# Sample attention moved beside prompt attention, in plain fp32 on quarter arrays

## The chip, the core and the metric

The kernel runs on one core of one Trainium2 chip. Its engines work from queues of their own and wait for each other by semaphores: TensorE (PE, with its weight loads shown as PEld), VectorE (DVE), ScalarE (ACT), GpSimd (POOL) and SyncE (SP), which here issues nearly all DMAs. The metric is the device time of one execution in microseconds.

## The reference

A two-layer decoder trunk serves a prompt of 1024 new tokens and 8 sample requests of 4 new tokens each. Layer 0 is a causal convolution module, layer 1 is forgetting attention with 16 heads of 64; each is followed by a SwiGLU FFN. The change is in layer 1, behind the joint projection of q, k, v and the log forget values:

```python
def fox_prompt(q, k, v, logf):            # 1024 queries over 1024 keys, causal, blocks of 128 queries
    c = jnp.cumsum(logf, axis=1)
    s = einsum('bqhd,bkhd->bhqk', qi, k) * scale + ci[..., None] - cT[:, :, None, :]
    pr = softmax(where(kpos <= qpos, s, -inf)); return einsum('bhqk,bkhd->bqhd', pr, v)

def fox_sample(q, k, v, logf, cache_k, cache_v, cache_logf, page_table):
    kp = cache_k[page_table].reshape(DB, P, H, dh)    # 8 pages of 128 rows for each of 8 requests
    vp = cache_v[page_table].reshape(DB, P, H, dh)
    # the same attention of 4 new queries over 1024 cached rows and themselves
```

A cache page is 128 rows x 1024 values of fp32, 512 KB for the keys and as much for the values; 64 pages of each are read.

## The kernel before, in words

All work is laid out by hand: each engine has one queue, written in order, and waits where the code says so. The kernel goes through the stages one after the other: convolution, FFN, attention projection, prompt attention, sample attention, output projection, FFN, final norm. Projections multiply with operands split into a high and a low fp32r part (three products, lines 749 to 751). The weights of a projection pass through two buffers `wraw`; ACT casts each to `whi` (line 1184) and POOL subtracts it into `wlo` (line 655).

*Prompt attention* takes the 16 heads as 8 pairs, and each pair in 8 slots: query tiles of 128 rows, from tile 7 (1024 keys) down to tile 0 (128 keys). For slot n PE computes the scores of both heads, one on the upper and one on the lower 64 rows of the array (`scores_pair`, line 1024), into banks 0 to 3. DVE adds the cumulated log forget values and takes the negated row maximum in one instruction (`tile_max`, line 1823), POOL having put the causal mask on the diagonal block (line 714). ACT takes the exponential into `pr` (line 1458). In the next slot PE transposes `pr` block by block (`probs_tr`, line 995) into banks 4 and 5, from which DVE and ACT copy it to `pt` (lines 1814 and 1444). A slot later PE multiplies with the values (`values`, line 1041), each head in its own 64 columns of the array, into bank 6 or 7. When a half of a pair (four tiles) is done, the reciprocal sums are spread by a transpose (line 1007), copied to `R`, and applied on the way to `OT` (line 1831). The order of PE's queue and the last wait of `scores_pair` are

```python
            for n in range(NSLOT + 2):
                early = n < NSLOT and query_tile(n) < 3
                ... scores_pair(n), probs_tr(n - 1, 0), probs_tr(n - 1, 1), scale_tr ...
                if n >= 2:
                    values(n - 2)
                past(pe, a_exp, 2 * (n - 1) if qt < 3 else 2 * n)
```

where for the wide tiles `scores_pair` stands behind the first head's transposes, and for tiles 2 to 0 (`early`) ahead of them.

*Sample attention* starts when all of that is done (`sp.wait_ge(a_pv, NSLOT)`). Per request, the 8 key pages are loaded into four buffers `kr`, transposed on PE (line 1075), split into `KTh` by ACT (1480) and `KTl` by DVE (1877), and multiplied with queries spread over 64 rows, high and low part side by side (1088, 1089). The exponential (1510) is transposed (1105), split again, and multiplied with value pages split into `Vh` by ACT (1488) and `Vl` by POOL (722), in products of 128 x 512 (1116, 1117), 1122 adding the new tokens. Of the 64 x 1024 results PE selects each head's own columns (`select`, line 1130). The values of a request are taken while the keys of the next are. Then `OT` is split into `xhi` and `xlo` and the output projection starts. Its first two weight units have been loaded and split ahead.

Of the kernel before, what the change touches and what calls it, by code (L numbers as in the profile page):

```python
# [34 lines left out]
ds = bass.ds  # L35
# [5 lines left out]
def hybrid_step(nc, x_prompt, x_sample, state_conv, cache_k, cache_v, cache_logf, page_table,  # L41
# [35 lines left out]
    with ExitStack() as ctx:  # L77
# [83 lines left out]
        own = at("own", [P, C, H], F32, after("newqk"))  # L161
        isum = at("isum", [P, 64], F32, after("own"))
        NMT = at("NMT", [H * TNEW, NREQ, NS], F32, after("isum"))
# [11 lines left out]
        NM = at("NM", [NS, NREQ, H, TNEW], F32, after("csumt"))  # L175
# [5 lines left out]
        smx = at("smx", [H * TNEW, 1], F32, after("rden"))  # L181
        sden = at("sden", [H * TNEW, 1], F32, after("smx"))
        srd = at("srd", [P, 1], F32, after("sden"))
# [5 lines left out]
        qa = at("qa", [P, 2, SEQ], F32, where["xhi"][0])  # L189
        ka = at("ka", [P, 2, SEQ], F32, after("qa"))  # L190
        cb = at("cb", [P, 2, 2, SEQ], F32, after("ka"))
# [3 lines left out]
        pt = at("pt", [P, 2, 2, SEQ], F32, where["stg"][0])  # L195
# [7 lines left out]
        kr = at("kr", [P, 4, D], F32, where["stg"][0])  # L203
        assert after("kr") <= where["newqk"][0]
        KTh = at("KTh", [P, 2, C, 2 * P], FR, H0)
        KTl = at("KTl", [P, 2, C, 2 * P], FR, after("KTh"))
        assert after("KTl") <= where["kr"][0]
        vr = at("vr", [P, 2, D], F32, where["xhi"][0])

        vr2 = at("vr2", [P, 2, D], F32, where["wraw"][0])  # L210
        Vh = at("Vh", [P, 2, D], FR, after("vr"))
        Vl = at("Vl", [P, 2, D], FR, after("Vh"))

        cbx = at("cbx", [H * TNEW, PAST], F32, after("Vl"))

        qs = at("qs", [P, C, P], FR, after("cbx"))
        assert after("qs") <= where["xlo"][0]
        qx = at("qx", [P, C, H, TNEW], F32, where["NM"][0])

        S = at("S", [H * TNEW, PAST + NS], F32, where["rs"][0])  # L220
        Pm = at("Pm", [H * TNEW, PAST + NS], F32, where["sq"][0])
        PTs = at("PTs", [P, NPG, P], FR, where["tm"][0])
        PTn = at("PTn", [NS, P], F32, where["fz"][0])
        ob = at("ob", [P, D], F32, where["csumt"][0])
# [75 lines left out]
        x_mm = sem("x_mm")  # L300
        x_ev = sem("x_ev")
        a_ld = [sem("a_ld0"), sem("a_ld1")]
        a_sc = sem("a_sc")
        a_mask = sem("a_mask")
        a_mx = sem("a_mx")
        a_exp = sem("a_exp")
# [1687 lines left out]
```

## Time and profile before

| | |
|---|---|
| median of 3 runs | 3156.82 us (3156.65 to 3157.34) |
| the profiled execution | 3151.71 us, its span 3150.0 us |
| busy in the span | PE 2858.6 us (91%), DVE 1121.6, ACT 962.5, POOL 967.3 |
| mean granted TensorE clock | 0.953 of full speed |
| HBM | 191.48 MB read, 23.13 MB written |

A span is the time from the first to the last instruction that the profiler recorded. Busy times of matmuls are modelled, since they are pipelined: a matmul's row includes its way through the array, and the distance between the starts of two weight loads or matmuls tells what one costs in a stream. A plain fp32 matmul is recorded as two passes, so the counts of such rows are twice the matmuls. "Idle before <- releaser" is the time that an engine had stood idle ahead of a row, and who ended it. [...]

### The profile page before, as it was taken

How to read it: one execution, taken by the hardware profiler on the slowest of the kernel's cores; microseconds unless marked ns; L12 is line 12 of the kernel's file. 1: busy time of each engine (PE TensorE's matmuls, PEld its weight loads, DVE VectorE, ACT ScalarE, POOL GpSimd, SP SyncE). 2: the span in 40 equal slices, each digit the busy share in tenths (PEclk: the TensorE clock that was granted, in tenths of full speed). 3: DMA queues.
4: the chain of work that ended last, by engine and by line, in shares of the span. 5: the costliest groups of instructions: out<-in, count | busy, mean ns of one | idle time of the engine just before them, and what ended most of it. 6: DMA issues, size and time to landing. Idle time of an engine off the chain costs nothing.

```text
span 3150.0 us, 48571 instructions
## 1 busy us (share of the span) xinstructions
PE 2858.6 (91%) x17970; PEld 2661.0 (84%) x17970; DVE 1121.6 (36%) x1820; ACT 962.5 (31%) x1549; POOL 967.3 (31%) x564
## 2 busy tenths in 40 slices
PE   5887698999999999899988888998989999999997
PEld 4787497999999999799975556886879999999997
DVE  6999634111111112511126665553351111111114
ACT  4555523211112112302124544554232111111123
POOL 2899323222222222312112212556131221212211
PEclk8898799999999999999999998988899999999998
DMA  3101011111111111224222114775111111111111
GB/s 97 40 27 40 15 47 34 37 50 47 34 54 37 50 47 34 62 70 129 72 74 110 55 55 166 275 251 189 41 38 42 40 47 43 44 47 36 52 36 72
DMA packets 244634, 215.16 MB, mean 68 GB/s; under 512 B 18108, under 2 KB 218812, under 8 KB 243492
## 3 DMA queue, kind: packets, MB, share of 16 engines
q1 hardware_dynamic: 231399, 194.98, 19.7%
q10 hardware_dynamic: 13133, 18.80, 1.8%
q8 instruction: 65, 1.06, 0.1%
q14 instruction: 37, 0.30, 0.0%
HBM read 191.48 MB, written 23.13 MB: 68 GB/s over the span
## 4 chain that ended last, share of the span: by engine, by line
PE 74%; DVE 15%; issue 5%; ACT 3%; DMA 1%; POOL 1%; DVEq 0%; SPq 0%; ACTq 0%; POOLq 0%
PE PS L749 20%; PE PS L751 20%; PE PS L750 20%; DVE PS L1685 6%; PE PS L1024 3%; DVE tm L1574 2%; PE PS L995 2%; PE PS L1041 1%; PE PS L1075 1%; DVE rs L1553 1%; PE PS L1116 1%; PE PS L1117 1%; PE PS L1088 1%; PE PS L1089 1%; DMA xin<-in_x_prompt 1%
## 5 line engine op out<-in xcount | busy, mean ns | idle before, releaser
L749 PE MATMUL PS<-xhi,whi 128*128 128x352 f32 x3456 | 1144.0, 331 | 118.3 <-DVE u L1663 40.5
L751 PE MATMUL PS<-xlo,whi 128*128 128x352 f32 x3456 | 1120.8, 324 | 0.0
L750 PE MATMUL PS<-xhi,wlo 128*128 128x352 f32 x3456 | 1120.7, 324 | 0.0
L655 POOL TENSOR_TENSOR wlo<-wraw,whi 128x1024 fp32r<-128x1024 f32 x208 | 496.9, 2390 | 1605.6 <-ACT whi L1184 1605.6
L749 PEld LDWEIGHTS PS<-xhi,whi 128*128 128x128 f32 x3456 | 657.4, 190 | 161.9 <-DVE hlo L1616 48.1
L750 PEld LDWEIGHTS PS<-xhi,wlo 128*128 128x128 f32 x3456 | 660.4, 191 | 0.0
L751 PEld LDWEIGHTS PS<-xlo,whi 128*128 128x128 f32 x3456 | 658.2, 190 | 0.0
L1184 ACT ACTIVATE whi<-wraw 128x1024 fp32r<-128x1024 f32 x208 | 218.9, 1052 | 595.4 <-PE PS L751 566.9
L1611 DVE TENSOR_TENSOR ht<-PS,ht 128x352 f32<-128x352 f32 x132 | 69.1, 524 | 906.1 <-PE PS L751 902.1
L749 PE MATMUL PS<-hhi,whi 128*128 128x352 f32 x1056 | 341.2, 323 | 8.8 <-issue 8.8
L750 PE MATMUL PS<-hhi,wlo 128*128 128x352 f32 x1056 | 338.5, 321 | 0.0
L751 PE MATMUL PS<-hlo,whi 128*128 128x352 f32 x1056 | 338.2, 320 | 0.0
L1597 DVE TENSOR_TENSOR X<-PS,X 128x352 f32 x216 | 113.2, 525 | 445.8 <-PE PS L751 445.4
L749 PEld LDWEIGHTS PS<-hhi,whi 128*128 128x128 f32 x1056 | 198.1, 188 | 10.8 <-issue 10.8
L750 PEld LDWEIGHTS PS<-hhi,wlo 128*128 128x128 f32 x1056 | 198.4, 188 | 0.0
L751 PEld LDWEIGHTS PS<-hlo,whi 128*128 128x128 f32 x1056 | 197.9, 187 | 0.0
L1685 DVE SCALAR_TENSOR_TENSOR PS<-u,par,PS 128x1024 f32<-128x1024 f32 x152 | 195.9, 1289 | 4.8
L722 POOL TENSOR_TENSOR Vl<-vr,Vh 128x1024 fp32r<-128x1024 f32 x64 | 151.7, 2384 | 137.2 <-ACT Vh L1488 137.2
L1239 ACT ACTIVATE hhi<-ht 128x352 f32 x132 | 65.5, 498 | 410.3 <-DVE ht L1611 410.3
L677 POOL TENSOR_TENSOR yp<-yp,prods 128x1024 f32<-128x1024 f32 x72 | 172.3, 2393 | 10.3
L1233 ACT ACTIVATE ht<-PS 128x352 f32<-128x352 f32 x132 | 60.8, 464 | 367.5 <-PE PS L751 367.4
L1286 ACT ACTIVATE prods<-u,par 128x1024 f32<-128x1024 f32 x88 | 99.6, 1149 | 113.2 <-POOL yp L677 68.8
(198 smaller groups left out, 2816.1 us busy)
## 6 DMA issues: line engine op xcount, KB each, us to landing
wraw<-in_ffn_w_gu SPq DMA_DIRECT2D x88, 512.0 KB, 3.8
kr<-in_cache_k SPq DMA_DIRECT2D x64, 512.0 KB, 5.1
vr<-in_cache_v SPq DMA_DIRECT2D x64, 512.0 KB, 5.1
wraw<-in_ffn_w_down SPq DMA_DIRECT2D x32, 384.0 KB, 3.3
wraw<-in_attn_w_in SPq DMA_DIRECT2D x24, 512.0 KB, 3.9
wraw<-in_ffn_w_down SPq DMA_DIRECT2D x32, 320.0 KB, 3.0
wraw<-in_conv_w_in SPq DMA_DIRECT2D x16, 512.0 KB, 4.0
cb<-c_scr SPq DMA_DIRECT2D x8, 1024.0 KB, 7.6
```

The source lines that it names most:

```text
L655: nc.gpsimd.tensor_tensor(wlo[:, s, :], wraw[:, s, :], whi[:, s, :].bitcast(F32), ALU.subtract).then_inc(w_lo, 1)
L677: nc.gpsimd.tensor_tensor(yp[:, :], prods[:, 0, :] if i == 1 else yp[:, :], prods[:, i % 3, :], ALU.add).then_inc(p_tap, 1)
L722: nc.gpsimd.tensor_tensor(Vl[:, j % 2, :], raw_values(j), Vh[:, j % 2, :].bitcast(F32), ALU.subtract).then_inc(v_lo, 1)
L749: nc.tensor.matmul(out, wh, hi[:, k, blk(b)], start=(k == 0), stop=False)
L750: nc.tensor.matmul(out, wl, hi[:, k, blk(b)], start=False, stop=False)
L751: m = nc.tensor.matmul(out, wh, lo[:, k, blk(b)], start=False, stop=(k == kc - 1))
L1024: m = nc.tensor.matmul(PS[:, score_banks(n, s) + k0 // 512, 0:k1 - k0], qa[rows, i % 2, qt * P:(qt + 1) * P], ka[rows, i % 2, k0:k1], star ...
L1184: nc.scalar.activation(whi[:, s, :], wraw[:, s, :], ACT.Copy).then_inc(w_hi, 1)
L1286: nc.scalar.activation(prods[:, i % 3, :], u[:, k:k + SEQ], ACT.Copy, scale=par[:, q, R_DW + k:R_DW + k + 1]).then_inc(a_tap, 1)
L1597: nc.vector.tensor_tensor(xs, PS[:, NB * s + b, 0:BW], xs, ALU.add).then_inc(ev[s], 1)
L1611: nc.vector.tensor_tensor(ht[:, b, :], PS[:, NB + b, 0:BW], ht[:, b, :], ALU.mult).then_inc(ev[1], 1)
L1685: nc.vector.scalar_tensor_tensor(acc, u[:, k:k + SEQ], tap(k), acc, ALU.mult, ALU.add).then_inc(cv, 1)
```

## The change

The sample stage goes, and its work is put into the prompt slots, in steps: step m transposes key page m, takes the scores of page m - 1, and the value products of page m - 11 (`LAG`). A slot does one step, the seventh slot of each pair two: 72 steps in the 64 slots, 4 more behind them. The splits are gone. Scores and values are plain fp32 matmuls on 32 columns of the array: four groups g of 32 columns hold the 16 heads, 4 heads by 4 new tokens in a group, with two matmuls (e = 0, 1) accumulated per group for the scores of a page, and one per group for its values (256 columns). Banks 4 and 5 are now filled alternately by a list (`fills`) that holds the prompt transposes (P), the spread sums (R), page scores (S, SN for the new tokens), the two halves of a page's transposed keys (K), the transposed probabilities of a request (T, TN) and the selection (O); a fill waits until the fill two places ahead has been copied out, by DVE or by ACT as listed. `pt` has one buffer in place of two, and `values(n - 1)` runs in slot n in place of `values(n - 2)`. Of two buffers for the queries of a pair one is left, and of two for its keys one and a half. The key pages (three buffers), the value pages (two) and `cbx` lie where `wraw`, `whi` and `wlo` are, so the weights of the output projection are loaded when the last key page has been transposed, and cast when the last value product is done. The transposition of the new tokens' mask, 8 transposes, becomes 32 small fp32 matmuls.

PE's queue, for the 768-key tile of the third head pair, from its scores to the value products of the tile before. Before:

```order
L1024 MATMUL PS<-ka,qa 128x512 [waits a_exp]
L1024 MATMUL PS<-ka,qa 128x512
L1024 MATMUL PS<-ka,qa 128x256 x2
L995 MATMUL PS<-ident,pr 128x128 [waits a_ptv,a_exp]
L995 MATMUL PS<-ident,pr 128x128 x3
L995 MATMUL PS<-ident,pr 128x128 [waits a_pta]
L995 MATMUL PS<-ident,pr 128x128 x2
L1041 MATMUL PS<-pt,Vt 64x128 [waits a_pta,a_ptv,o_ev]
L1041 MATMUL PS<-pt,Vt 64x128 x15
```

After, from the second half of the second head's transposes on (ahead of it stand the same scores, now from `kl` and `kh`):

```order
L1035 MATMUL PS<-ident,pr 128x128 [waits a_pta]
L1035 MATMUL PS<-ident,pr 128x128 x2
L1102 MATMUL PS<-KT,qs 32x128 [waits a_pta,a_ptv]
L1102 MATMUL PS<-KT,qs 32x128 x7
L1121 MATMUL PS<-ident,kr 128x128 [waits a_pta,k_ld2]
L1121 MATMUL PS<-ident,kr 128x128 x3
L1121 MATMUL PS<-ident,kr 128x128 [waits a_ptv]
L1121 MATMUL PS<-ident,kr 128x128 x3
L1133 MATMUL PS<-vr,PT 32x256 [waits v_ld1]
L1133 MATMUL PS<-vr,PT 32x256 x3
L1085 MATMUL PS<-pt,Vt 64x128 [waits a_pta,a_ptv]
L1085 MATMUL PS<-pt,Vt 64x128 x13
```

Behind the probabilities there are now, ahead of the value products, the page scores (KT, qs), both halves of the key transposes (kr), of which the second waits for DVE (a_ptv), and the page values (vr, PT).

DVE's queue in the same slot. Before:

```order
L1814 COPY pt<-PS 128x512 [waits a_pv,a_tr]
L1823 ISA PS,nmx<-PS,cb 128x768 [waits a_mask,a_sc]
L1823 ISA nmx 128x1
L1814 COPY pt<-PS 128x512 [waits a_pv,a_tr]
L1823 ISA PS,nmx<-PS,cb 128x768 [waits a_mask,a_sc]
L1823 ISA nmx 128x1
```

After (smx and S are the running maximum and the scores of the request):

```order
L1838 COPY pt<-PS 128x512 [waits a_pv,a_tr]
L1847 ISA PS,nmx<-PS,cb 128x768 [waits a_mask,a_sc]
L1847 ISA nmx 128x1
L1847 ISA PS,nmx<-PS,cb 128x768 [waits a_mask,a_sc]
L1847 ISA nmx 128x1
L1881 ISA S,smx<-PS,cbx 128x128 [waits a_tr]
L1881 ISA smx 128x1
L1902 COPY KT<-PS 128x512 [waits a_tr] x2
```

The second copy of probabilities has moved to ACT, and behind both maxima stand the exit of the page's scores and the two copies of its transposed keys.

```diff
+        kr = at("kr", [P, 3, D], F32, where["wraw"][0])
+        vr = at("vr", [P, 2, D], F32, after("kr"))
+        cbx = at("cbx", [P, PAST], F32, after("vr"))
+        assert after("cbx") <= where["xhi"][0]
+        KT = at("KT", [P, C, P], F32, after("cb"))
+        assert after("KT") <= where["xlo"][0]
...
+        NPAGE = NREQ * NPG
+        LAG = NPG + 3
+        NSTEP = NPAGE + LAG + 1
+        NALL = NSLOT + 4
+        def steps_before(n):
+            return n + min(n // NT + (1 if n % NT > 6 else 0), C)
+        def sample_steps(n):
+            return range(steps_before(n), min(steps_before(n + 1), NSTEP))
...
+        def fills():
+            for n in range(NALL):
+                if 1 <= n <= NSLOT:
+                    wide = query_tile(n - 1) >= 4
+                    yield ("P", n - 1, 0, 0), ON_DVE
+                    if wide:
+                        yield ("P", n - 1, 0, 1), ON_ACT
+                    yield ("P", n - 1, 1, 0), ON_ACT
+                    if wide:
+                        yield ("P", n - 1, 1, 1), ON_ACT
+                    if halves_ended(n - 1):
+                        yield ("R", (n - 1) // 4), ON_DVE
+                for m in sample_steps(n):
+                    if 1 <= m <= NPAGE:
+                        yield ("S", m - 1), ON_DVE
+                        if (m - 1) % NPG == 0:
+                            yield ("SN", (m - 1) // NPG), ON_DVE
+                    if m < NPAGE:
+                        yield ("K", m, 0), ON_DVE
+                        yield ("K", m, 1), ON_DVE
...
+        def bank(key):
+            return 4 + fill[key] % 2
+        def emptied(eng, u):
+            engine, n = filled_by[u]
+            eng.wait_ge(a_ptv if engine == ON_DVE else a_pta, n)
...
+            def load_k(p):
+                if p >= 3:
+                    bank_full(sp, ("K", p - 3, 1))
+                v = page(p)
+                sp.dma_start(kr[:, p % 3, :], cache_k[0][ds(v, 1)].rearrange("a p h d -> p (a h d)")
+                             ).then_inc(k_ld[p % 3], 16)
+            def load_v(p):
+                if p >= 2:
+                    sp.wait_ge(v_mm, p - 1)
+                v = page(p)
+                sp.dma_start(vr[:, p % 2, :], cache_v[0][ds(v, 1)].rearrange("a p h d -> p (a h d)")
+                             ).then_inc(v_ld[p % 2], 16)
...
                 if n % 4 == 0:
-                    past(pe, o_ev, hh - 1)
+                    past(pe, o_ev, hh)
                 for kb in range(qt + 1):
                     for s in range(2):
-                        m = nc.tensor.matmul(PS[DH * s:DH * s + DH, 6 + hh % 2, (qt % 4) * P:(qt % 4 + 1) * P],
+                        m = nc.tensor.matmul(PS[DH * s:DH * s + DH, 6, (qt % 4) * P:(qt % 4 + 1) * P],
                                              Vt[:, kb, i * P + s * DH:i * P + s * DH + DH],
-                                             pt[:, n % 2, s, kb * P:(kb + 1) * P],
+                                             pt[:, s, kb * P:(kb + 1) * P],
                                              start=(kb == 0), stop=(kb == qt))
                 m.then_inc(a_pv, 1)
-            for n in range(NSLOT + 2):
+            def page_scores(p):
+                b, j = divmod(p, NPG)
+                if j == 0:
+                    pe.wait_ge(d_q, b + 1)
+                evacuated(pe, ("K", p, 0))
+                evacuated(pe, ("K", p, 1))
+                u = ("S", p)
+                bank_free(pe, u)
+                for e in range(2):
+                    for g in range(4):
+                        m = nc.tensor.matmul(PS[NS * g:NS * g + NS, bank(u), 0:P], qs[:, b % 2, 2 * g + e, :],
+                                             KT[:, 2 * g + e, :], start=(e == 0), stop=(e == 1))
+                m.then_inc(a_tr, 1)
...
+            def page_tr(p):
+                pe.wait_ge(k_ld[p % 3], 16 * (p // 3 + 1))
+                for half in range(2):
+                    u = ("K", p, half)
+                    bank_free(pe, u)
+                    for c in range(4):
+                        m = nc.tensor.transpose(PS[:, bank(u), c * P:(c + 1) * P],
+                                                kr[:, p % 3, (4 * half + c) * P:(4 * half + c + 1) * P], ident[:, :])
+                    m.then_inc(a_tr, 1)
+            def page_values(p):
+                b, j = divmod(p, NPG)
+                if j == 0:
+                    evacuated(pe, ("TN", b))
+                    past(pe, d_ob, b)
+                pe.wait_ge(v_ld[p % 2], 16 * (p // 2 + 1))
+                for g in range(4):
+                    m = nc.tensor.matmul(PS[NS * g:NS * g + NS, 7, 0:2 * P], PT[:, j, NS * g:NS * g + NS],
+                                         vr[:, p % 2, 2 * P * g:2 * P * (g + 1)], start=(j == 0), stop=False)
...
+                m.then_inc(v_mm, 1)
...
+            def sample_step(m):
+                if 1 <= m <= NPAGE:
+                    page_scores(m - 1)
+                if m < NPAGE:
+                    page_tr(m)
+                if LAG <= m < NPAGE + LAG:
+                    page_values(m - LAG)
+                if m >= LAG - 1 and (m - LAG + 1) % NPG == 0 and m - LAG + 1 < NPAGE:
+                    sample_tr((m - LAG + 1) // NPG)
+                if m >= LAG + NPG and (m - LAG) % NPG == 0:
+                    select((m - LAG) // NPG - 1)
+            for n in range(NALL):
                 early = n < NSLOT and query_tile(n) < 3
                 if early:
                     scores_pair(n)
@@ -1056,107 +1189,13 @@
                     probs_tr(n - 1, 1)
                     if halves_ended(n - 1):
                         scale_tr((n - 1) // 4)
-                if n >= 2:
-                    values(n - 2)
+                for m in sample_steps(n):
+                    sample_step(m)
+                if 1 <= n <= NSLOT:
+                    values(n - 1)
...
+            act.wait_ge(v_mm, NPAGE)
+            for s in range(2):
+                hi_part(Q_ATTN_OUT, s)
+            evacuated(act, ("O", NREQ - 1))
...
-                for a, u in enumerate(tr_units(n)[s]):
-                    if u % 2:
-                        continue
-                    dve.wait_ge(a_tr, u + 1)
-                    past(dve, a_pv, n - 1)
-                    k0, k1 = 512 * a, min(nk, 512 * a + 512)
-                    nc.vector.tensor_copy(pt[:, n % 2, s, k0:k1], PS[:, 4 + u % 2, 0:k1 - k0]).then_inc(a_ptv, 1)
+                u = tr_units(n)[s][0]
+                bank_full(dve, u)
+                past(dve, a_pv, n)
+                k1 = min(nk, 512)
+                nc.vector.tensor_copy(pt[:, s, 0:k1], PS[:, bank(u), 0:k1]).then_inc(a_ptv, 1)
...
+            def page_out(p):
+                b, j = divmod(p, NPG)
+                u = ("S", p)
+                bank_full(dve, u)
...
+                nc.vector.tensor_tensor_reduce(S[:, b % 2, j * P:(j + 1) * P], PS[:, bank(u), 0:P],
+                                               cbx[:, j * P:(j + 1) * P], 1.0, -3.0e38, ALU.add, ALU.max,
+                                               accum_out=smx[:, b % 2, j:j + 1]).then_inc(a_ptv, 1)
...
+            def keys_in(p):
+                if p >= 1:
+                    bank_full(dve, ("S", p - 1))
+                for half in range(2):
+                    u = ("K", p, half)
+                    bank_full(dve, u)
+                    nc.vector.tensor_copy(KT[:, 4 * half:4 * half + 4, :],
+                                          PS[:, bank(u), :].rearrange("p (c f) -> p c f", f=P)).then_inc(a_ptv, 1)
...
+            for n in range(NALL):
+                ended = 1 <= n <= NSLOT and halves_ended(n - 1)
+                if 1 <= n <= NSLOT:
+                    probs_out(n - 1, 0)
...
+                if n < NSLOT:
+                    for s in range(2):
+                        tile_max(n, s)
+                if ended:
+                    bank_full(dve, ("R", hh))
+                    past(dve, o_ev, hh)
+                    nc.vector.tensor_copy(R[:, :], PS[:, bank(("R", hh)), :]).then_inc(a_ptv, 1)
+                if 2 <= n < NSLOT + 2 and halves_ended(n - 2):
+                    half_out((n - 2) // 4)
+                for m in sample_steps(n):
+                    sample_step(m)
...
```

## Rows read from the trace of the kernel before

**Rows 1.** Windows: engines' busy us (instructions), granted clock, DMA share, GB/s.
```profile
1629.74:1919.20 289.46, 246.71 (x2165) 164.54 (x2165) 176.71 (x407) 145.03 (x360) 56.77 (x126) 0.97 0.16 62
1919.20:2217.48 298.28, 269.18 (x1654) 225.18 (x1653) 141.29 (x172) 146.40 (x165) 151.73 (x64) 0.83 0.69 236
1776.09:1811.28 35.19, 30.03 (x273) 20.23 (x273) 22.13 (x52) 18.04 (x46) 7.20 (x16) 1.00 0.16 61
2000.00:2150.00 150.00, 145.44 (x926) 123.67 (x925) 80.35 (x96) 79.86 (x90) 83.90 (x36) 0.87 0.77 266
```

**Rows 2.** Waits of DVE and ACT, prompt stage: us in total, times, longest.
```profile
DVE PS L1823 <- PE PS L1024: 76.5, 48, 4.5
...
ACT pr L1458 <- DVE nmx L1823: 106.8, 79, 3.9
```

**Rows 3.** Timeline, one turn of a 768-key tile: start us, us, engine, instructions.
```profile
1680.38 1.56 PE L1024 MATMUL PS<-ka,qa 64*128 64x512 f32 x8 [0.57 <-ACT pr L1458]
1681.87 0.75 PEld L995 LDWEIGHTS PS<-ident,pr 128*128 128x128 f32 x7 [0.33 <-issue]
1681.97 0.97 DVE L1823 CUSTOM_DVE_ANT_0 PS<-PS,cb 128x768 f32<-128x768 f32 x1 [1.64 <-PE PS L1024]
1682.79 1.73 PEld L1041 LDWEIGHTS PS<-pt,Vt 128*64 128x64 f32 x32 [0.17 <-issue]
1682.86 0.69 DVE L1814 COPY pt<-PS 128x512 f32<-128x512 f32 x1
1683.46 0.96 DVE L1823 CUSTOM_DVE_ANT_0 PS<-PS,cb 128x768 f32<-128x768 f32 x1
1684.33 0.14 DVE L1823 DVE_READ_ACCUMULATOR2_ANT nmx<- 128x1 f32 x1
1684.51 0.90 ACT L1458 ACTIVATE pr<-PS,nmx 128x768 f32<-128x768 f32 x1
1685.31 0.19 ACT L1458 ACTIVATION_READ_ACCUMULATOR pr<-PS,nmx 128x1 f32 x1
1685.55 0.30 PEld L1024 LDWEIGHTS PS<-ka,qa 64*128 64x128 f32 x4 [0.23 <-ACT pr L1458]
```

**Rows 4.** Groups by line and shape, prompt stage: count, busy us, mean ns.
```profile
L1823 DVE CUSTOM_DVE_ANT_0 PS<-PS,cb 128x1024 f32<-128x1024 f32 x16 | 19.6, 1230 | 12.4 <-PE PS L1024 12.4
L1444 ACT ACTIVATE pt<-PS 128x512 f32<-128x512 f32 x24 | 14.3, 594 | 24.2 <-PE PS L995 24.2
L1823 DVE CUSTOM_DVE_ANT_0 PS<-PS,cb 128x128 f32<-128x128 f32 x16 | 4.7, 294 | 3.9 <-PE PS L1024 3.9
```

**Rows 5.** Timeline: scores of 1024 and 128 keys, four transposes and their copy.
```profile
1629.74 1.99 PE L1024 MATMUL PS<-ka,qa 64*128 64x512 f32 x8 [1.33 <-DVE NMT L1793]
...
1672.21 0.66 PE L995 MATMUL PS<-ident,pr 128*128 128x128 f32 x4 [1.30 <-ACT pr L1458]
1672.90 0.69 DVE L1814 COPY pt<-PS 128x512 f32<-128x512 f32 x1 [0.65 <-PE PS L995]
...
1700.34 0.49 PE L1024 MATMUL PS<-ka,qa 64*128 64x128 f32 x4
```

**Rows 6.** Timeline, PE: undivided passes of small and of large matmuls.
```profile
1617.92 1.03 PE L932 MATMUL PS<-ident,newqk 128*32 128x128 f32 x8 [0.40 <-ACT Vt L1408]
...
1627.97 0.44 PE L982 MATMUL PS<-ident,NM 32*64 32x32 f32 x8
...
2042.67 1.98 PE L1122 MATMUL PS<-vnew,PTn 32*128 32x512 f32 x4
```

**Rows 7.** Timeline: the first output-projection matmul.
```profile
2217.48 0.63 PE L749 MATMUL PS<-xhi,whi 128*128 128x352 f32 x1 [1.68 <-DVE xlo L1946]
```

**Rows 8.** DMA issues: KB each, median us to landing.
```profile
kr<-in_cache_k SPq DMA_DIRECT2D x64, 512.0 KB, 5.1
```

**Rows 9.** Groups by line: cast of a weight unit and its low part.
```profile
L655 POOL TENSOR_TENSOR wlo<-wraw,whi 128x1024 fp32r<-128x1024 f32 x208 | 496.9, 2390 | 1605.6 <-ACT whi L1184 1605.6
L1184 ACT ACTIVATE whi<-wraw 128x1024 fp32r<-128x1024 f32 x208 | 218.9, 1052 | 595.4 <-PE PS L751 566.9 <-DMA wraw<-in_attn_w_in 25.7 <-DMA wraw<-in_conv_w_in 2.8
```

More of the change, by code:

```diff
@@ L406, in score_banks, with evacuated, bank_free, bank_full @@
             return 2 * s + (1 if qt in (2, 0) else 0)
-        def evacuated(eng, u):
-            if u >= 0:
-                eng.wait_ge(a_ptv if u % 2 == 0 else a_pta, u // 2 + 1)
+        fill, filled_by, count = {}, [], [0, 0]
+        for key, engine in fills():
+            count[engine] += 1
+            fill[key] = len(filled_by)
+            filled_by.append((engine, count[engine]))
+        def bank(key):
[3 more added lines that the diff above has]
+            eng.wait_ge(a_ptv if engine == ON_DVE else a_pta, n)
+        def evacuated(eng, key):
+            emptied(eng, fill[key])
+        def bank_free(eng, key):
+            if fill[key] >= 2:
+                emptied(eng, fill[key] - 2)
+        def bank_full(eng, key):
+            eng.wait_ge(a_tr, fill[key] + 1)
+        def tr_units(n):
+            return [[("P", n, s, a) for a in range(2 if query_tile(n) >= 4 else 1)] for s in range(2)]
         def banks(first, n):
@@ new lines, in select @@
+            def select(b):
+                u = ("O", b)
+                pe.wait_ge(d_ob, b + 1)
+                bank_free(pe, u)
+                for e in range(2):
+                    m = nc.tensor.matmul(PS[:, bank(u), NS * e:NS * e + NS], ob[:, e * P:(e + 1) * P],
+                                         ident[:, :].rearrange("p (g x) -> p g x", g=4)[:, :, 8 * e:8 * e + 8],
+                                         start=True, stop=True)
+                m.then_inc(a_tr, 1)
+            def sample_step(m):
[5 more added lines that the diff above has]
+                    page_values(m - LAG)
+                if m >= LAG - 1 and (m - LAG + 1) % NPG == 0 and m - LAG + 1 < NPAGE:
+                    sample_tr((m - LAG + 1) // NPG)
+                if m >= LAG + NPG and (m - LAG) % NPG == 0:
+                    select((m - LAG) // NPG - 1)
@@ L1079, in scores @@
-            def scores(b, g):
-                pe.wait_ge(k_lo, b * NPG + (2 * g + 2))
-                if g == 0:
-                    pe.wait_ge(d_q, b * 2 + 2)
-                    past(pe, d_s, b * 4)
-                out = PS[:, 4 + g // 2, (g % 2) * 2 * P:(g % 2 + 1) * 2 * P]
-                for c in range(C):
-                    nc.tensor.matmul(out, qs[:, c, :], KTh[:, g % 2, c, :], start=(c == 0), stop=False)
-                    m = nc.tensor.matmul(out, qs[:, c, :], KTl[:, g % 2, c, :], start=False, stop=(c == C - 1))
-                m.then_inc(k_sc, 1)
@@ L1150, in _ @@
-            request(0, False, False)
-            request(1, True, False)
-            with pe.Fori(2, NREQ) as b:
-                request(b, True, True)
-            select(NREQ - 2)
-            exp_tr(NREQ - 1)
-            for j in range(NPG):
-                values_page(NREQ - 1, j)
-            select(NREQ - 1)
-            pe.wait_ge(d_o, 2 * NREQ)
+            evacuated(pe, ("O", NREQ - 1))
             def attended(b, k):
```

573 lines of the change are left out of this document (231 added, 342 removed).

## The prediction

> **What bounds the kernel now.** I read the page's forty slices first, then the stages by window, then who waits for whom in the first of them, then one turn of its loop in the timeline. Two stages are touched. Prompt attention runs from 1629.74 to 1919.20 us and sample attention from there to 2217.48, where the first output-projection matmul starts: 289.5 + 298.3 = 587.7 us [rows 1, 7]. In the sample stage PE shows busy for 269 of 298 us: PE-bound, at a mean granted clock of 0.83. In the prompt stage no engine is full, DVE has 177 of 289 us and ACT 145. There DVE's row maxima wait 76.5 us for the scores and ACT's exponentials 106.8 us for the maxima [rows 2]: a chain of handovers. One turn shows it [rows 3]: scores of the 768-key tile start at 1680.38, the two maxima at 1681.97 and 1683.46, the second exponential is read out at 1685.50, and only then (1685.55) do the next scores start. 5.17 us a turn; PE's transposes and value products lie inside the waits. So the prompt stage has room on every engine, and the question is what order the new work takes in it.
>
> **The change, part by part.** *Removed:* the separate sample stage, 298.3 us, with the hi/lo splits of keys and values on ACT, DVE and POOL. *Added to each prompt turn:* one page step on PE (page scores, 8 key transposes, page values), on DVE one score exit and two key copies. ACT gets one exponential and three copies per request. There are 64 slots and 72 page steps in them (the seventh slot of each pair has two), then four closing steps.
>
> What an added PE pass costs. A plain fp32 matmul shows two passes. With 512 moving columns and the array not divided by columns, a pass starts each 0.43 us (four in 1.98 us with the tail) [rows 6], so 0.107 us per 128 columns. The value products, in two column halves, take 32 passes of 128 columns in 1.73 us, 0.054 us each [rows 3]: two run side by side. No row shows four side by side. The lower end is four: 0.027 us per 128-column pass, and 32-column passes do start about 0.036 us apart, (0.44 - 0.19)/7 with 0.19 the tail of one [rows 6]. The upper end is one at a time: 32-column weights by themselves take 0.107 us per pass, eight in 1.03 us with the tail [rows 6]. Nothing excludes a value between; I take the end nearest the half-array row, four, with page scores 16 x 0.032 = 0.5 us and page values 8 x 0.054 = 0.43 us. One at a time each would be 1.72 us. [...]
>
> Where it lies. Three orders decide. PE now issues, per turn: first-head transposes, scores, second-head transposes, page scores, key halves K0 and K1, page values, value products of the tile before. All fills of banks 4 and 5 alternate strictly, so K1 waits until DVE has taken the page's scores out. And DVE takes them out behind both maxima. So the loop closes anew: scores, max, max, score exit, K1, page values, value products, first-head transposes, scores. The exponentials, which closed the loop before, get cover. Behind the waiting K1 in PE's queue stand the page values, the value products and the next scores, and for those wait DVE and ACT.
>
> The closing run per step, at the higher clock: score exit 0.29 us plus the accumulator read, 0.35 in all [rows 4]; hop 0.05; four key transposes 4 x 0.107 = 0.43; change of array division 0.17 (the idle time ahead of the value products [rows 3]); page values 0.43; 0.17; value products 0.216 per key block of the tile before; 0.17; transposes 0.107 per block; 0.2 to the scores (0.23 in [rows 3]). Without the two block terms that is 1.97. Ahead of it: scores to first maximum 1.59 us at 768 keys, one step of 128 keys 0.215 (1.99 us of scores at 1024, 0.49 at 128 [rows 5]); two maxima, 1.23 us each at 1024 and 0.29 at 128 [rows 4], less the 0.08 overlapped with the read.
>
> In three slots of eight (768, 640 and 512 keys) the page scores are late, not the maxima: they wait for ACT's copy of the second head, which for 768 starts 1.49 + 0.69 us after the scores ([rows 3]; four transposes to their copy in [rows 5]), takes 0.59 [rows 4], and is followed by 0.17 + 0.5 + 0.27 of page scores: exit at about 3.8 us instead of 3.4. Where a half ends, a copy of R or the OT product (0.69 us each) stands in DVE's queue ahead of the exit.
>
> Slot by slot from 1024 to 128 keys I get 8.1, 9.1, 7.9, 7.4, 6.7, 6.7, 7.8 (two page steps) and 4.4 us: 58.1 per pair, against 35.19 at full clock now [rows 1]. The present stage takes 289.46/8 = 36.18 per pair, a factor 1.028 for dips of the clock; so 59.7. Pair 0 has no page values yet (9 x 0.6 less: 54.3), pair 1 two fewer (58.5), five pairs at 59.7, and the last has no key page left and stays near the old loop, 40: together 451. Per request once: 9 transposes 0.96, their three alternating fills behind ACT 0.9, scores of the new tokens 0.35, selection 0.6, exponential, reciprocal and copies about 0.7 in queue: 3.5 x 8 = 28. Start: 32 small matmuls in place of 8, and DVE now waits for the store of the cumulated sums before its first maximum: 3 us. End: values of page 63 can only be loaded when page 61 has been used; a page takes 5.1 us to land [rows 8], and behind the last product stand the first weight cast, 1.05 us, and POOL's difference, 2.39 [rows 9], no longer done ahead because their buffers hold pages: 10.5 us. In all 451 + 28 + 3 + 10.5 = 492.5 us in place of 587.7.
>
> Costed at nothing: page loads. Keys are issued three pages ahead and values about two turns ahead, against 5.1 us to land; 1 MB per turn of 7 us is 150 GB/s where the sample stage moved 236 [rows 1]. Without that cover each page would add up to 5 us. POOL's mask (0.46 us) stays inside the maxima. Later stages are the same code.
>
> Sum: 3151.71 - 95 = 3056.7 us for an execution like the profiled one; the median of the runs, 3156.82, is 5.1 above it, so 3062.
>
> **Rivals.**
> *Quarter arrays only two at a time.* Then page scores and values take 0.86 us each: 0.43 on the loop, and of the other 0.36 about 0.14 a step on average, since only three slots wait for it. 0.57 x 64 = 37 us later: 3099. For it: the trace shows a factor of two and no more. Against: 32-column passes can start every 0.036 us.
> *One at a time, slower than before.* 1.29 us more page values on the loop, 1.2 more page scores of which the maxima cover a third: 2.1 x 64 = 134 us, 3196. It wins over the gain from 95/64 = 1.5 us a page on. Against: the half tiles do overlap; for: weights of 32 columns alone bring nothing in [rows 6].
> [...]
> *More is hidden than I count.* If the request work fits the waits and the page scores never decide, 28 + 10 us go: 3024.
>
> **How the numbers follow.** Main forecast 0.62; two at a time 0.11; clock 0.11; more hidden 0.08; one at a time 0.05; other ways to be slower (a page load uncovered, a clock of 0.8 or below) 0.03. The likeliest alone spans 3035 to 3095, from a loop 5% shorter or longer (22 us) and 10 us in the ends. The range 3015 to 3130 takes in the first three rivals that make it faster. A time within 0.2% (6.3 us), about what a measurement of this kernel can tell from no change, needs nearly the whole gain lost: 0.03. Faster 0.89, slower 0.08.
>
> **What would show it.** Right: no sample stage behind prompt attention; 58 to 61 us from one 1024-key score to the next in the middle pairs; PE's second key half waiting for DVE's 128-column score exit, and ACT no longer the one that releases the scores; page values 0.45 to 0.6 us a page; the first output-projection matmul near 2122 us; about 10 us between the last prompt tile and it. Wrong: page values near 0.9 or 1.7 us; PE waiting for a page's DMA in the middle; a granted clock under 0.9 in the stage; a pair under 54 us or over 64.

## The result: 2.3% faster, some 20 us short of the forecast

The changed kernel takes 3082.85 us (median of 4 runs, 3079.12 to 3089.54) against 3157.08 us for the kernel before, timed beside it: a ratio of 0.9767, 95% interval 0.9749 to 0.9786. The forecast was 3062 us; 95 us were to go, 74 went. The profiled execution lasts 3085.33 us, its span 3083.2 us.

A stage is counted here from its own first prompt scores, which the kernels below reach at 1627.3 to 1633.5 us, to the first output-projection matmul. Windows of the changed kernel, columns as in [rows 1]: the whole stage, then the third, the fifth and the sixth pair of heads (from first 1024-key scores to first 1024-key scores), and the end, from the first value products behind the last slot on.

```profile
1633.48:2147.73 514.25, 425.31 (x4520) 279.10 (x4521) 273.89 (x706) 178.65 (x433) 59.82 (x128) 0.94 0.52 175
...
1756.51:1829.42 72.91, 60.24 (x616) 39.25 (x615) 36.12 (x94) 22.98 (x56) 7.43 (x16) 0.88 0.52 170
...
1894.50:1959.08 64.58, 53.84 (x598) 35.53 (x598) 35.74 (x92) 21.69 (x53) 7.19 (x16) 0.97 0.52 184
1959.08:2019.91 60.83, 52.81 (x598) 34.63 (x597) 35.55 (x92) 21.68 (x53) 7.19 (x16) 1.00 0.59 194
...
2134.80:2147.73 12.93, 5.89 (x41) 2.06 (x41) 3.90 (x8) 4.01 (x8) 2.88 (x2) 0.50 0.45 137
```

The two stages of [rows 1] took 587.7 us together; the one stage takes 514.3 where 492.5 were forecast. The row that answers to [rows 7] starts at 2147.73 (forecast "near 2122"); 3.7 us of the difference lie ahead of the stage. From the transposes of the new tokens, which are the same in both kernels, to the first scores it is 11.83 us here and 11.82 before (1617.92 in [rows 6], 1629.74 in [rows 5]):

```profile
1621.65 1.03 PE L970 MATMUL PS<-ident,newqk 128*32 128x128 f32 x8 [0.40 <-ACT Vt L1447]
...
1633.48 1.13 PE L1067 MATMUL PS<-kl,qa 64*128 64x512 f32 x4 [1.03 <-DVE NMT L1819]
```

Against the forecast, with the 3.5 us of a request in each pair: start 0.0 us (3), pair 0 55.4 (57.8), pair 1 67.7 (62.0), pairs 2 to 6 together 328.7 (316.0), the last 49.6 (43.5), end 12.9 (10.5). So pairs 1 to 6 lack 18 us, the last one 6.

First, a slot that nothing disturbs. Timeline of the changed kernel, the 896-key tile of pair 4 (columns as in [rows 3]):

```profile
1902.64 1.13 PE L1067 MATMUL PS<-kl,qa 64*128 64x512 f32 x4
...
1904.44 1.10 DVE L1847 CUSTOM_DVE_ANT_0 PS<-PS,cb 128x896 f32<-128x896 f32 x1 [1.44 <-PE PS L1067]
...
1905.46 1.13 DVE L1847 CUSTOM_DVE_ANT_0 PS<-PS,cb 128x896 f32<-128x896 f32 x1
...
1905.78 0.64 PE L1102 MATMUL PS<-KT,qs 128*32 128x128 f32 x16 [0.34 <-ACT pt L1485]
...
1906.51 0.68 DVE L1855 TENSOR_TENSOR OT<-PS,R 128x512 f32<-128x512 f32 x1
...
1907.11 0.28 DVE L1881 CUSTOM_DVE_ANT_0 S<-PS,cbx 128x128 f32<-128x128 f32 x1
...
1907.46 0.66 PE L1121 MATMUL PS<-ident,kr 128*128 128x128 f32 x4 [0.45 <-DVE smx L1881]
...
1908.04 0.64 PE L1133 MATMUL PS<-vr,PT 128*32 128x256 f32 x8
...
1911.43 1.13 PE L1067 MATMUL PS<-kl,qa 64*128 64x512 f32 x4
```

8.79 us from scores to scores, forecast 9.1. The second key half (L1121) waits for the score exit (L1881), which stands behind both maxima and the OT product: the loop of the forecast, in its order. The page values (L1133) last 0.64 us with their tail, and ACT no longer releases the scores, as it did in [rows 3].

Now where the time is. Waits of PE in the stage (us in total, times, longest):

```profile
PE PS L1121 <- DVE smx L1887: 23.6, 8, 5.5
PE PS L1121 <- DVE R L1960: 12.8, 12, 1.8
PE PS L1102 <- ACT pt L1485: 9.8, 22, 0.6
PE PS L1102 <- DVE pt L1838: 8.5, 21, 0.4
PE PS L1133 <- DMA vr<-in_cache_v: 5.9, 3, 3.6
PE PS L1121 <- DVE smx L1881: 5.5, 12, 0.5
```

The first row is in no term of the forecast: eight waits, one for each request, for the exit of its new-token scores (L1887), which stands behind the exit of its first page (L1881). Timeline of the changed kernel at one of them, ahead of the fourth request:

```profile
1809.22 0.29 DVE L1881 CUSTOM_DVE_ANT_0 S<-PS,cbx 128x128 f32<-128x128 f32 x1
...
1811.01 0.33 SPq L594 DMA_DIRECT2D kr<-in_cache_k  x1
1811.39 2.66 SPq L610 DMA_DIRECT2D cbx<-cb_scr  x4
...
1811.93 0.34 PE L1110 MATMUL PS<-newqk,qs 128*32 128x32 f32 x16
...
1817.34 0.29 DVE L1881 CUSTOM_DVE_ANT_0 S<-PS,cbx 128x128 f32<-128x128 f32 x1 [6.10 <-issue]
...
1817.79 1.94 PE L1121 MATMUL PS<-ident,kr 128*128 128x128 f32 x8 [5.52 <-DVE smx L1887]
```

The exit adds the request's cumulated log-forget sums, and cbx holds those of one request. Its reload may begin only when the last page of the request before has left (1809.22). SP gets to it behind a key page, 1.9 us after that exit has ended, and issues four transfers one after the other (2.66 us); DVE goes on 5.95 us after the first was issued. The new request's scores have been in PSUM since 1812.3; DVE waits, PE behind it. The profile names no releaser for this wait ("issue"). Of the seven waits of this kind in the stage it names the transfer for the two short ones (DVE's waits; us in total, times, longest):

```profile
DVE S L1881 <- issue: 19.5, 5, 6.1
...
DVE S L1881 <- DMA cbx<-cb_scr: 2.6, 2, 1.4
```

That it is the transfer in the other five too is an inference up to here, which the first experiments test. After the wait, in which PE stood for 5.5 us, the eight key transposes take 1.94 us, against 1.14 in an undisturbed slot: the granted clock is down, 0.50 from 1817.8 to 1819.8, 0.88 over this pair, 1.00 over pair 5.

### The profile page after: what moved, and what is told of

Same layout as the page of the kernel before. It is cut to its first block, busy times and chain, and to the rows that moved or that the text cites. A ratio compares the mean times of both kernels' runs of the same rounds, so it can differ in the third digit from the quotient of the medians.

```text
span 3083.2 us, 49477 instructions
## 1 busy us (share of the span) xinstructions
PE 2770.7 (90%) x18730; PEld 2554.4 (83%) x18730; DVE 1079.6 (35%) x1948; ACT 847.5 (27%) x1453; POOL 817.3 (27%) x500
## 4 chain that ended last, share of the span: by engine, by line
PE 75%; DVE 16%; issue 4%; ACT 3%; DMA 1%; POOL 1%; SPq 0%; DVEq 0%; ACTq 0%; POOLq 0%
PE PS L787 21%; PE PS L789 20%; PE PS L788 20%; DVE PS L1709 6%; PE PS L1067 2%; PE PS L1085 2%; PE PS L1121 2%; DVE tm L1598 2%; PE PS L1035 2%; DVE rs L1577 1%; PE PS L1133 1%; DVE PS L1847 1%; PE PS L1102 1%; DMA xin<-in_x_prompt 1%; DVE hlo L1640 1%
## 5 line engine op out<-in xcount | busy, mean ns | idle before, releaser
L763 POOL TENSOR_TENSOR cb<-cb,cmask 128x128 f32<-128x128 f32 x128 | 57.8, 459 | 449.7 <-DVE nmx L1847 440.8
L1485 ACT ACTIVATE pt<-PS 128x512 f32<-128x512 f32 (+3 forms) x128 | 57.7, 476 | 287.6 <-PE PS L1035 287.6
```

## The experiments

### The sums loaded once, and loaded in halves

One kernel loads for the first request alone. The other loads all, in two halves of the columns:

```
                 if b >= 1:
-                    evacuated(sp, ("S", b * NPG - 1))
+                    evacuated(sp, ("S", b * NPG - 1 - NPG // 2 * (1 - half)))
...
+                if p % NPG == 7 and (p + 1) // NPG < NREQ:
+                    load_sums((p + 1) // NPG, 0)
                 if p % NPG == 3 and 1 <= p // NPG < NREQ:
-                    load_sums(p // NPG)
+                    load_sums(p // NPG, 1)
...
-                    dve.wait_ge(cb_ld, 64 * (b + 1))
+                    dve.wait_ge(cb_ld[j // 4], 64 * (b + 1))
```

Once: 

> The four transfers that fill cbx are issued for the first request alone; the other seven use its sums (their sample outputs are other numbers). Theory, the reload of cbx is the missed term: in the changed kernel DVE stands 1.2 to 6.1 us ahead of the first page-score exit of each request, and PE 23.6 us in 8 waits for that exit. All of it goes and nothing else is late in its place: 20 to 35 us off, 3048 to 3063 us. Rival, the slots with two steps are long because PE's and DVE's queues hold more work there (new-token scores, transposes of the probabilities, the scale rows), and the transfer lands beside it: within 8 us of the changed kernel, 3075 to 3085 us.

Halves: 

> cbx is filled in two halves: columns of pages 0 to 3 as soon as page 3 of the request before has left it, four steps ahead of their use, columns of pages 4 to 7 where the whole was filled; 8 transfers of 32 KB a request instead of 4 of 64 KB, nothing left out. Theory, the reload is the missed term: the first half has some 25 us and the second one some 25 us of cover, so as much is gained as by no reload, within 6 us of that kernel (3050 to 3068 us). Rival, what costs is the SP queue that issues them, not the wait for the single buffer: four more issues a request of some 0.65 us each ahead of page loads, 3080 to 3095 us.

Measured: 3054.42 us, ratio 0.9689 (0.9673 to 0.9705), and 3052.89 us, 0.9677 (0.9661 to 0.9693). The intervals lie wholly below that of the changed kernel; the halves take 0.0090 x 3157 = 28 us off. The stage with the halves:

```profile
1627.77:2117.36 489.59, 415.76 (x4521) 272.78 (x4521) 273.30 (x706) 178.43 (x433) 59.66 (x128) 0.97 0.54 184
```

PE's waits in it:

```profile
PE PS L1125 <- DVE R L1965: 12.8, 12, 1.8
PE PS L1106 <- ACT pt L1489: 9.8, 22, 0.6
PE PS L1137 <- DMA vr<-in_cache_v: 9.8, 6, 3.7
PE PS L1106 <- DVE pt L1842: 8.7, 21, 0.4
...
PE PS L1125 <- DVE smx L1892: 2.9, 6, 1.0
```

The wait for the new-token exit goes from 23.6 to 2.9 us, the stage from 514.3 to 489.6, 2.9 us under the forecast, and its clock from 0.94 to 0.97, as forecast. Of the 24.7 us 15.1 are PE's idle time (20.7 us less at this exit, 3.9 more for value pages), and 9.6 its busy time, for the same work (4520 and 4521 records): that part goes with the clock. The reload is the missed term; the rival (longer queues in the slots with two steps) is out.

### The value products in one column group

```
-                    m = nc.tensor.matmul(PS[NS * g:NS * g + NS, 7, 0:2 * P], PT[:, j, NS * g:NS * g + NS],
+                    m = nc.tensor.matmul(PS[0:NS, 7, 0:2 * P], PT[:, j, NS * g:NS * g + NS],
...
```

The products of the new tokens are changed in the same way.

> The value products of the pages and of the new tokens all write the same 32 rows of the bank, added up over the four groups (the sample outputs are other numbers); in the changed kernel each of the four has 32 rows of its own. Theory, the four quarter arrays run at once: 16 passes of 256 columns one behind the other are 4 x 0.43 = 1.7 us a page instead of 0.43, and they stand in the loop of a slot, so 64 x 1.3 = 83 us slower where all of it shows and 40 where half is hidden: 3120 to 3170 us. Rival, the groups run one after the other already: within 5 us of the changed kernel.

Measured: 3157.80 us, 1.0011 (1.0002 to 1.0021): 77 us slower than the changed kernel, so the whole gain gone by this one edit. PE, the same eight passes (a plain fp32 matmul is two records: the 64 x 4 page matmuls of L1133 are 512 in either kernel, the 576 value products of L1041 in the kernel before 1152):

```profile
1912.15 1.91 PE L1133 MATMUL PS<-vr,PT 128*32 128x256 f32 x8
```

1.91 us in place of 0.64; 72 times (8 for the new tokens) 1.27 are 91 us, of which 77 show. One pass takes 0.22 us here (in the page before, the eighth starts 1.54 us behind the first); the last lasts 0.38. Two in a row would so end after 0.22 + 0.38 = 0.60 us (an estimate), and 0.64 is what the four groups take side by side. So four run at once, to within 0.04 us.

### Nothing beside prompt attention

```
         def steps_before(n):
-            return n + min(n // NT + (1 if n % NT > 6 else 0), C)
+            return NSTEP if n > NSLOT + 2 else 0
...
```

SP's loads follow that order: the prompt's first, then the pages.

Apart: 

> All 76 steps of sample attention stand behind the last query tile of prompt attention, in the same form (plain fp32, quarter arrays, the same buffers); nothing runs beside prompt attention. Theory, the gain comes from standing beside it: the prompt stage goes back to some 290 us, and the steps alone are bound by the page loads, 1 MB a page at the 236 GB/s of the sample stage before, 4.4 us x 64 = 284 us and some 36 for the requests: 3140 to 3180 us, about the kernel before. Rival, the form alone is the gain (no split of keys and values into parts, a page step of some 3 us: copies 0.69 x 2, scores 0.5, exit 0.3, products 0.43): 64 x 3 + 36 = 228 us, 3090 to 3100 us.

Apart, with the sums in halves: 

> All steps of sample attention behind prompt attention as before, with the sums loaded in halves. In the run with the whole reload DVE stood 51.3 us in 6 waits and 5.7 us in one ahead of a request's first exit, and PE 42.6 us for value pages. Theory, the page loads are the bound of steps that stand alone: part of the 57 us of the reload turns into waits for pages; 64 MiB of pages at 300 GB/s are 224 us instead of the 298 of the stage, with the prompt stage at 330: 3130 to 3165 us. Rival, the steps run at the 2.73 us of the undisturbed ones, 76 x 2.73 = 207 us and 4 us a request: 3110 to 3130 us.

Measured: 3207.09 us, 1.0177 (1.0154 to 1.0201), and 3192.15, 1.0131 (1.0110 to 1.0152). Both slower than the kernel before, and further than either theory said. The prompt stage and the sample stage of the second:

```profile
1627.26:1959.60 332.34, 257.01 (x2179) 173.48 (x2180) 160.08 (x383) 154.53 (x385) 56.37 (x126) 0.93 0.18 65
1959.60:2254.32 294.72, 196.37 (x2345) 124.72 (x2342) 116.60 (x324) 24.41 (x47) 2.88 (x2) 0.83 0.69 234
```

PE's longest wait in the latter:

```profile
PE PS L1130 <- DMA vr<-in_cache_v: 68.7, 40, 3.3
```

Two things follow. Standing alone, the new form of sample attention is hardly faster than the old (294.7 against 298.3 us): it has less to compute (PE 196.4 us busy against 269.2) and waits for its value pages instead, and its end holds the first weight cast, which the kernel before had done ahead. That its mean rate, 234 GB/s, is near the 236 of [rows 1] says nothing by itself, since both move the same pages in nearly the same time, and from 2040 to 2050 us this run moves 317 GB/s. Whether the rate or the short lead of two value buffers sets the wait was not tested. And the new prompt order by itself is 43 us slower than the old, 332.3 against 289.5. Some 10 us of that are PE's busy time (257.0 against 246.7, at a clock of 0.93 in place of 0.97), the rest waits. Those between 1700 and 1900 us, in the first of the two kernels, say where:

```profile
PE PS L1078 <- DVE OT L1848: 19.4, 10, 2.0
PE PS L1078 <- ACT pt L1478: 14.5, 20, 0.8
```

Its value products (L1078) wait for two things, 29.2 and 24.1 us over the whole prompt stage. They have one bank (6) where the kernel before had two (6 and 7), so a half of a pair begins only when DVE's OT product has emptied it; and they follow their own tile's transposes at once and wait for the copies, where before they were those of the tile before. The kernel before shows no wait of its value products (L1041) in that stage. This is read from the traces and was not tested by itself. So all of the gain comes from standing beside: 332.3 + 294.7 = 627.1 us apart become 489.6 beside.

### What closes the loop

On top of the halves. Maxima over 512 keys: `nk = min((query_tile(n) + 1) * P, 512)` in the maxima alone.

> As the kernel with the halves, but the maxima and the added bias take only the first 512 keys of a tile (the prompt outputs are other numbers). Theory of the forecast, both maxima of a slot stand in the loop that sets its length (scores, max, max, score exit, second key half): 2 x (1250 - 711) ns less in a slot of 1024 keys, 0.81, 0.54 and 0.28 us in those of 896, 768 and 640, 2.7 us a pair, 21 us in all: 3031 us. Rival, PE is the bound and what it waits for between the tiles is the scalar engine's last copy of pt, which gives the bank of the page scores back (0.45 us ahead of them in a slot of 768 keys); the maxima run beside: 3048 to 3056 us.

Score exit between the maxima:

```
                 if n < NSLOT:
-                    for s in range(2):
-                        tile_max(n, s)
+                    tile_max(n, 0)
                 if ended:
...
+                if between:
+                    for m in sample_steps(n):
+                        if 1 <= m <= NPAGE:
+                            page_out(m - 1)
+                if n < NSLOT:
+                    tile_max(n, 1)
```

> As the kernel with the halves, but in the slots with one step DVE takes the exit of the page scores between the two maxima, and R's copy ahead of it; the amount of work is the same. Theory of the forecast, the second maximum leaves the loop: 1.25, 1.12, 0.98, 0.85, 0.71, 0.58 and 0.31 us in the seven slots of a pair, up to 46 us off; half of it where something else is next: 3007 to 3030 us. Rival, the page scores are not there when the first maximum ends (in a slot of 768 keys they end 0.06 us behind the second one), so DVE waits for them with the second maximum behind, which has some 4 us before the next slot's transposes need it: 3046 to 3060 us.

Page scores ahead of the second head's transposes on PE, exit between the maxima on DVE:

```
+                if ahead(n):
+                    page_scores(ahead(n) - 1)
                 if 1 <= n <= NSLOT:
                     probs_tr(n - 1, 1)
```

> As the kernel with the halves, but in slots with one step (those of a request's first page left out) PE takes the page scores between the prompt scores and the transposes of the second head's probabilities, and DVE their exit between the two maxima; the order in which the two banks rotate follows. Theory, PE is the bound: its wait of 0.45 us for the copy of pt and of 0.2 us for the score exit go in each wide slot, and a wait of up to 0.3 us for the exit comes ahead of the second head's second block: 0.3 to 0.5 us in some 48 slots, 15 to 25 us off: 3028 to 3040 us. Rival, the loop through the maxima: the second maximum leaves it as well, over 30 us off: below 3020 us. Rival on the other side, the two banks now hold the score exit ahead of the transposes and every slot waits for DVE there: 3055 to 3080 us.

Measured: 3037.84 us, 0.9639 (0.9621 to 0.9656); 3041.37, 0.9650 (0.9630 to 0.9670); 3041.97, 0.9647 (0.9629 to 0.9665). Against the halves 12, 9 and 9 us by the ratios; the first interval lies under that of the halves, the other two overlap it. The stages of the profiled runs shrink by 19.1, 13.7 and 12.8 us. With the short maxima PE's waits are these:

```profile
PE PS L1106 <- ACT pt L1489: 9.8, 22, 0.6
PE PS L1137 <- DMA vr<-in_cache_v: 9.5, 5, 3.6
PE PS L1106 <- DVE pt L1842: 8.7, 21, 0.4
PE PS L1125 <- DVE R L1965: 6.4, 12, 0.8
```

The maxima are on the loop in part: 19.1 of 21 us in the profiled stages, 12 by the ratios, and 6.4 us of it are less wait for R's copy, which stands behind the maxima. The waits for the copies of pt (18.5 us in 43) don't move. The exit between the maxima, with R's copy moved as well (its wait falls to 5.7 us), gains far less than the 46 us of a second maximum, since the page scores aren't there yet. DVE at a 640-key tile of that kernel:

```profile
1891.62 0.83 DVE L1851 CUSTOM_DVE_ANT_0 PS<-PS,cb 128x640 f32<-128x640 f32 x1 [0.80 <-PE PS L1071]
...
1893.65 0.29 DVE L1886 CUSTOM_DVE_ANT_0 S<-PS,cbx 128x128 f32<-128x128 f32 x1 [1.14 <-PE PS L1106]
```

Neither theory holds by itself: two chains, maxima to score exit and pt's copies to page scores, end close to each other (0.06 us in the slot of 768 keys that the expectation names), so taking one away shows the other. The third edit shortens both, and new waits come in their place. PE's waits with the page scores ahead:

```profile
PE PS L1134 <- DVE R L1979: 5.6, 12, 0.6
...
PE PS L1060 <- DVE smx L1897: 4.7, 6, 0.8
...
PE PS L1115 <- DVE pt L1853: 3.7, 9, 0.4
PE PS L1134 <- ACT pt L1500: 3.3, 12, 0.4
```

At the page scores (L1115) PE waits 4.6 us for copies of pt in place of 18.5, and 5.6 in place of 12.8 for R's copy; but it now waits 3.3 us for ACT's copies at the key transposes (L1134) and 4.7 for the score exit at the spreading of the sums (L1060). That the two chains limit each other is read from these rows; no run takes both away.

With R's copy ahead of the second maximum too: 

> As the kernel with the page scores ahead, but in the slots that end a half of eight tiles DVE takes R's copy ahead of the second maximum too. Theory, PE is the bound of the stage and waits 5.6 us in 12 turns and 1.9 us in two for R's copy, in which the second maximum stands ahead of it by 0.7 or 1.25 us: 4 to 8 us less than the kernel with the scores ahead, 3034 to 3038 us. Rival, the second maximum is late then and with it the second head's exponentials, and the second head's transposes wait for them: 3040 to 3046 us.

Measured: 3046.74 us, 0.9655 (0.9642 to 0.9668): no gain over 0.9647. The rival held, in effect; where its time went was not followed further.

### The lead of the page loads

On top of the halves, two key buffers in place of three (`load_k` waits for page p - 2, not p - 3), and then the same with `load_v` ahead of `load_k` in SP's loop.

Two buffers: 

> As the kernel with the halves, with two buffers for key pages instead of three. Each key load is issued one step later, and as SP issues in order, all that is behind it too. Theory of the forecast, page loads cost nothing: a key page is still issued more than one slot (6.3 to 9 us) ahead against some 5 us to land, 3050 to 3056 us. Rival, the lead that hides them is thin: a value page would be issued one step ahead of its products, less than it takes to land where a slot lasts 4 to 5 us or holds two steps, 1 to 3 us late in some 16 steps: 3065 to 3085 us.

Values first: 

> As the kernel with two key buffers, but in each step SP issues the value page ahead of the key page, not behind it and the prompt's and the sums' transfers. Theory, what costs 80 us there is SP's order: value pages stand behind a key load that waits for a key buffer, and so get one step's lead; taken first they have two again, and the key loads keep their own: 3050 to 3060 us, as with three key buffers. Rival, two key buffers are too few by themselves, and key pages come late instead: 3110 to 3135 us.

Measured: 3132.35 us, 0.9930 (0.9909 to 0.9951), 80 us lost; and 3051.36, 0.9679 (0.9656 to 0.9701), all of it back. Two buffers: PE's wait for value pages in the stage, and the timeline where a request begins:

```profile
PE PS L1137 <- DMA vr<-in_cache_v: 65.8, 27, 5.9
...
1896.04 0.34 SPq L594 DMA_DIRECT2D kr<-in_cache_k  x1
1896.43 2.67 SPq L611 DMA_DIRECT2D cbx<-cb_scr  x4
...
1900.38 0.35 SPq L602 DMA_DIRECT2D vr<-in_cache_v  x1
...
1904.00 1.08 PE L1137 MATMUL PS<-vr,PT 128*32 128x256 f32 x8 [5.17 <-DMA vr<-in_cache_v]
```

Values first, the same wait:

```profile
PE PS L1137 <- DMA vr<-in_cache_v: 6.0, 3, 3.6
```

It was never the keys: value pages stand in SP's queue behind the key load that waits for a buffer, and lost one of two steps of lead with it. Both theories of the first run missed the size; the order of issue settles it.

The room of the third key buffer then takes a third value buffer, with the page scores ahead: 

> As the kernel with the page scores ahead, with two buffers for key pages and three for value pages in the same room, and value pages issued ahead of key pages. Theory, PE still waits 4 to 6 us in the middle and 5.6 us at the end for value pages, and nothing else stands there: 5 to 10 us less than the kernel with the scores ahead, a ratio of 0.9617 to 0.9633 to the kernel before, 3033 to 3040 us. Rival, what follows the last value products (the first weight cast and POOL's difference) sets the end whenever the page comes: no change, 0.9645 to 0.9657.

Measured: 3035.36 us, 0.9625 (0.9612 to 0.9638), the fastest of all: 3.7% under the kernel before, its interval wholly under that of the changed kernel. Against the scores ahead it is 7 us by the ratios, inside the 5 to 10 that were expected, though the two intervals overlap. PE's wait for value pages in the stage:

```profile
PE PS L1146 <- DMA vr<-in_cache_v: 2.4, 3, 1.8
```

## Why the forecast was right in its mechanism and short in its sum

- **The reload of the sums, a term that is missing.** "Per request once" lists transposes, fills, scores, selection, and comes to 3.5 us; "Costed at nothing: page loads" looks at keys and values. Neither has the transfer that comes once a request into a single buffer, and "PE waiting for a page's DMA in the middle" would not have shown it either. The sum had it at nothing; it is 28 us by the ratios, 24.7 in the profiled stages. With it hidden, the stage is 489.6 us against 492.5 and the kernel 3053 against 3062. That nearness is luck in part: start and pair 0 come out 6.3 us under their terms and the five middle pairs 6.8 (309.2 against 316.0), the last pair and the end 9.4 over (63.4 against 54.0).
- **Its own signs.** Two of the signs of being wrong did show: four of the five middle pairs took over 64 us (64.6 to 72.9), and the clock was 0.88 in one of them. Both went with the reload: with the halves these pairs take 60.0 to 63.3 us, where 59.7 and a request's 3.5 were forecast.
- **The start.** Forecast 3 us, measured nothing ahead of the first scores; DVE's wait for the store of the sums, 2.9 us, lies inside pair 0.
- **The loop.** Order and length held: undisturbed slots of 8.1, 8.8, 7.6, 7.1 and 6.8 us from 1024 keys to 512 in pair 4, against 8.1, 9.1, 7.9, 7.4 and 6.7. That the maxima close it is right by half. PE waits 5.5 us in 12 turns for the exit and 12.8 us in 12 for R's copy, both of which stand behind the maxima, but 18.3 us in 43 turns for the copies of pt, which the forecast gave three slots of eight.
- **Quarter arrays.** Four at once, as chosen from the half-array row; 0.64 us with the tail, inside the "0.45 to 0.6" but for it. The rival "one at a time", 83 us for the values alone, measures 77.
- **The last pair.** "Stays near the old loop, 40" took [rows 1] for the prompt order without pages. The new order alone runs 332.3/8 = 41.5 us a pair, and value pages and the last request come on top: 49.6.
- **The end.** 12.9 us against 10.5: the last value page is late by 3.6 us, the mechanism that was named (another is late by 2.0 us, still in the last pair). What PE waits for last is the split of OT (`xlo`, 2.78 us), not POOL's difference.
- **The clock.** 0.94 in place of 0.97, the lowest pair at 0.88. It is back at 0.97 in both runs without the waits for the sums. A stage at the 0.87 of [rows 1], from 2000 to 2150 us, did not come; what it would have cost, for which the chances hold 0.11, no run shows.
- **Page loads at nothing.** Right here, by one step: one step less costs 80 us.
- The stage gave 73.5 us, the span 66.8: this execution came to the stage 3.7 us later, and 2.9 us more pass behind the first projection matmul than before. Neither was followed.

## What to carry to other kernels

When work is moved beside other work, list every transfer it brings, the one per request as well as the one per page; here the reload of the single buffer cbx had too little time between the last read and the next. At the fourth request it took 2.66 us of issue and 5.95 us from the first issue to DVE's next read; DVE waited 1.2 to 6.1 us for it at seven requests, and halving it gained 28 us in all. Splitting that buffer by the order in which it is read gave the cover without more room: 3053 us, against 3054 with one load and 3083 with the whole reload. The page loads stand in SP's queue in order: value pages behind a key load that waits for its buffer cost 80 us, and ahead of it none, with the same buffers. So count leads in the queue and not in buffers.

## What was not expected of the hardware

- Four issues that broadcast into cbx (64 KB each) take SP 2.66 us, 0.67 each with what lies between them, where a page of 512 KB takes 0.33.
- Four 32-column tiles of fp32 weights run side by side: 0.64 us for 8 passes of 256 columns against 1.91 in one group.
- Alone, sample attention moves its pages at 234 GB/s and waits 68.7 us for them with PE busy 196 of 295 us; with less arithmetic that stage is only 4 us shorter. What sets the wait is open: 317 GB/s were reached within it.
